# A two-layer transformer block on one Trainium2 core: scores issued before a step's weight units instead of after them

## The reference

```python
# first block: three families of 8 heads each on one qkv product
y_a = diff_attention(q_a, k_a, v_a, lam, lam_init, diff_subln[l])   # two softmaxes per head, p0 - lam * p1
y_b = stick_breaking_attention(q_b, k_b, v_b, sb_norm[l])           # suffix sums of log(1 - beta)
y_c = chunk_band_attention(q_c, k_c, v_c, rel_bias[l], ch_norm[l])  # softmax with a relative bias
x = x + jnp.einsum('bse,ed->bsd', jnp.concatenate([y_a, y_b, y_c], axis=-1), w_o[l])
x = x + jnp.einsum('bsf,fd->bsd', jax.nn.silu(g) * u, w_down[l])    # g: a width-3 convolution of h @ w_gate
# second block
a = mla_mixer(c_q, c_kv, k_rope, positions, ...)                    # 8 heads, keys of 128 + 64
bb = dsa_mixer(q_d, k_d, v_d, q_idx, k_idx, w_idx, positions)       # 8 heads over 64 selected keys
x = x + jnp.concatenate([a, bb], axis=-1) @ w_out[l]
x = x + memory_cross_attention(hc, mem_n, ...)                      # 4 heads over 256 memory rows
x = x + jnp.square(jax.nn.relu(hm @ w_up[l])) @ w_down[l]
```

## Time and profile before

| | us |
|---|---|
| median of 3 timed runs | 2481.21 (2480.41 to 2484.02) |
| the profiled execution, its own time | 2483.1 |
| its span, first to last instruction | 2481.3 |
| VectorE busy | 1500.9 (60%) |
| ScalarE busy | 1261.0 (51%) |
| mean granted clock of TensorE | 0.992 |

### The profile page before, as it was taken

How to read it: one execution, slowest core, us unless ns; L and a number is a source line. 1 busy time by engine, 2 the same in 40 slices (tenths; PEclk the granted TensorE clock), 3 DMA queues, 4 the chain that set the end, 5 groups by cost and what they waited for, 6 DMA issues and landing times.

```text
span 2481.3 us, 31755 instructions
## 1 busy us (share of the span) xinstructions
PE 2417.3 (97%) x12304; PEld 2020.1 (81%) x12304; DVE 1500.9 (60%) x2311; ACT 1261.0 (51%) x1974; POOL 5.2 (0%) x12
## 2 busy tenths in 40 slices
PE   6999999999999999999999999999999999999998
PEld 5888887788888888888877877787788888888886
DVE  5586777666666556645667544564666556556454
ACT  5466566655555435534556445555544444344343
POOL 0000000000000000000000000000000000000000
PEclk9999999999999999999999999999999999999999
DMA  6544444455555665565454544554566666666664
GB/s 211 174 162 158 136 154 147 150 188 177 197 180 191 189 189 187 192 205 185 155 180 144 178 128 134 173 169 136 160 179 193 189 187 184 194 185 191 206 187 141
DMA packets 118341, 432.11 MB, mean 174 GB/s; under 512 B 13184, under 2 KB 13328, under 8 KB 117680
## 3 DMA queue, kind: packets, MB, share of 16 engines
q1 hardware_dynamic: 117216, 424.70, 54.7%
q0 software_dynamic: 976, 5.39, 0.6%
HBM read 427.93 MB, written 2.11 MB: 173 GB/s over the span
## 4 chain that ended last, share of the span: by engine, by line
PE 94%; DVE 2%; ACT 2%; issue 1%; DMA 1%; ACTq 0%; SPq 0%; DVEq 0%
PE bank L428 29%; PE bank L437 15%; PE bank L439 15%; PE bank L438 15%; PE bank L430 15%; PE bank L612 1%; PE bank L454 1%; DVE lo_w L1177 1%; ACT hi_w L771 0%; PE bank L596 0%; PE bank L485 0%; DVE xT L1300 0%; PE bank L566 0%; PE bank L575 0%; PE bank L523 0%
## 5 line engine op out<-in xcount | busy, mean ns | idle before, releaser
L1177 DVE TENSOR_TENSOR lo_w<-raw_w,hi_w 128x1024 fp32r<-128x1024 f32 x804 | 968.1, 1219 | 689.8 <-ACT hi_w L771 689.0
L771 ACT ACTIVATE hi_w<-raw_w 128x1024 fp32r<-128x1024 f32 x804 | 834.0, 1053 | 678.7 <-PE bank L439 429.7
L428 PE MATMUL bank<-xT,hi_w 128*128 128x512 f32 x3008 | 1062.6, 398 | 2.9 <-DVE lo_w L1177 1.8
L430 PE MATMUL bank<-xT,lo_w 128*128 128x256 f32 x3008 | 843.6, 280 | 0.0
L428 PEld LDWEIGHTS bank<-xT,hi_w 128*128 128x128 f32 x3008 | 566.3, 188 | 139.0 <-issue 2.1
L430 PEld LDWEIGHTS bank<-xT,lo_w 128*128 128x128 f32 x3008 | 569.3, 189 | 0.2
L439 PE MATMUL bank<-hi_w,act_lo 128*128 128x512 f32 x864 | 341.2, 395 | 0.0
L438 PE MATMUL bank<-lo_w,act_hi 128*128 128x512 f32 x864 | 341.2, 395 | 0.0
L437 PE MATMUL bank<-hi_w,act_hi 128*128 128x512 f32 x864 | 341.2, 395 | 0.0
L437 PE MATMUL bank<-hi_w,xT 128*128 128x512 f32 (+1 forms) x736 | 295.0, 401 | 4.2 <-DVE xT L1300 3.4
L439 PE MATMUL bank<-hi_w,xT 128*128 128x512 f32 (+1 forms) x736 | 287.6, 391 | 0.0
(11 more groups left out here) (299 smaller groups left out, 1486.6 us busy)
## 6 DMA issues: line engine op xcount, KB each, us to landing
raw_w<-in_w_up SPq DMA_DIRECT2D x216, 512.0 KB, 4.2
raw_w<-in_w_down SPq DMA_DIRECT2D x216, 512.0 KB, 4.2
raw_w<-in_w_gate SPq DMA_DIRECT2D x88, 512.0 KB, 3.6
raw_w<-in_w_in SPq DMA_DIRECT2D x72, 512.0 KB, 3.8
raw_w<-in_w_qk SPq DMA_DIRECT2D x64, 512.0 KB, 3.6
raw_w<-in_w_v SPq DMA_DIRECT2D x32, 512.0 KB, 3.7
raw_w<-in_w_o SPq DMA_DIRECT2D x32, 512.0 KB, 3.6
raw_w<-in_w_out SPq DMA_DIRECT2D x32, 512.0 KB, 3.6
```

Source lines behind the costliest of these rows:

```text
L428: e.matmul(pair[c][:, :], w_hi[:, cols_k], both[:, kt].rearrange("p h t -> p (h t)"), start=(kt == 0), stop=False, skip_group_check=True)
L430: last = e.matmul(pair[c][:, 0:TOK], w_lo[:, cols_k], both[:, kt, 0, :], start=False, stop=(kt == g.kts - 1), skip_group_check=True)
L771: e.activation(hi_w[:, u % SPLIT_SLOTS, 0:unit_cols[u]], raw_w[:, u % RAW_SLOTS, 0:unit_cols[u]], ACT.Copy).then_inc(s["w_hi"], 1)
L1177: e.tensor_tensor(lo, raw_w[:, u % RAW_SLOTS, 0:unit_cols[u]], hi.bitcast(F32), ALU.subtract).then_inc(s["w_lo"], 1)
```

## The change

In the step of every family TensorE now issues its scores behind values and transposes, and the step's units after them. Only TensorE's program changes; the others run their steps as before. Step 15 of mla keeps its order, since its scores read keys that are transposed in that step.

```diff
@@ attend @@
                         turn_tiles("k_d", staging, 8)
-                    units(fill[step])
+                        units(fill[step])
+                        scores(family, step)
+                        continue
                     if step < n:
                         scores(family, step)
+                    units(fill[step])
@@ diff @@
                 if 3 <= step < 19:
                     diff_turn(step - 3)
-                units(2)
                 if step < 16:
                     diff_scores(step)
+                units(2)
@@ sb, first pass @@
             for step in range(NH):
+                sb_scores(step, False)
                 units(step % 2)
-                sb_scores(step, False)
@@ sb, second pass @@
                 if 2 <= step < NH + 2:
                     sb_suffix(step - 2)
-                units((2, 2, 3, 2, 2, 3, 2, 3, 2, 2, 3)[step])
                 if step < NH:
                     sb_scores(step, True)
+                units((2, 2, 3, 2, 2, 3, 2, 3, 2, 2, 3)[step])
```

## The result

| | before | after |
|---|---|---|
| median of 4 timed runs, us | 2481.49 (2480.41 to 2484.02) | 2492.31 (2490.78 to 2494.14) |
| the profiled execution, its own time | 2483.1 | 2490.78 |
| its span | 2481.3 | 2489.0 |
| mean granted clock | 0.992 | 0.994 |

A forecast was written before the change was run, and what follows sets the result against it. TensorE was taken to bound the kernel; 8.7 (diff) + 0.4 (sb) + 1.0 (mla) + 1.1 (cross) - 0.2 (dsa) = 11.0 us gave 2494.1 us by the profile, 2492.2 against the median, range 2485 to 2498.

The forecast's parts named there:

- The bound: Whole kernel: TensorE, busy 97% of the span, bounds it; each microsecond it newly waits is a microsecond of kernel.
- The reordering by itself is worth nothing.: Seams of all loops: about 0.2 us saved and 0.2 paid in row changes per step, net 0.
- Group ends: diff steps 4, 6, 8, 14: scores wait for VectorE's maxima behind its add, 1.24 us each, 5.0 in all.
- Step 2: diff step 2: with no values or turn as cover, scores wait 1.7 us for VectorE's maxima.
- Step 10: diff step 10, no group end: VectorE's late split delays the maxima, so scores wait 0.6 us.
- Step 12: diff step 12: values wait for ScalarE's copy of the v group, no longer covered by scores, +0.7 us.
- Odd steps: diff odd steps: 0.7 us for steps 1 and 3 together, 0 from step 5 on.
- sb's first pass: sb's first pass: S(3) waits 1.5 us for a tanh, one seam saved gives 1.0 back, net +0.4 us.
- Entries: First scores directly behind their producer's copy or add: mla +1.0 us, cross +1.1, band 0; dsa may gain 0.2.
- (a): Rival, chance 0.14: VectorE runs ahead and absorbs most diff waits; 4.6 us lost in all, 2485.8 us.
- (b): Rival, chance 0.06, faster: scores after turn free, sb saves its seam, waits for turned weights go; 2474.6 us.
- (c): Rival, chance 0.14: granted clock falls behind diff's stalls; two or three falls +4 us (2496), all +14 (2506).

The follow-up runs named there:

- the shifted loop: The whole change with diff and sb loops shifted one unit against the groups of units, on all engines: 2486.82 us, ratio 1.0018 against the kernel before.

## Why the prediction was right, by its steps

- **The bound.** TensorE's time is the kernel's: 7.1 us of new waits in diff and 10.8 us of time. VectorE and ScalarE are as busy as before (60% and 51%), and taking TensorE's waits away gave the time back.
- **"The reordering by itself is worth nothing."** Shown within 0.04 us a step: 0.65 us over the 16 steps of diff with VectorE one step earlier, 0.3 over band's 16 (0 predicted; it comes in even pieces of 0.02 a step), and + 0.8 us for the whole change with nearly every wait taken out. S starts 0.20 us behind the last transpose and not 0.11, the full price of a change of rows.
- **Group ends, four times 1.24.** Measured 1.34. VectorE's side was exact (E + 1.72); the step from its maximum to TensorE's start took 0.15 us, where I had put 0.05. Two experiments that change only the distance between the engines (one unit ahead, and VectorE one step earlier) remove the wait.
- **Step 2, 1.7.** Measured 1.77. What I had left to a rival, a fall of the clock, followed it in two of three profiles with this wait, and cost 1.5 us in each by the drift. How much of the median it carries stays open, since the timed runs beside the profiled one have no record of where their clock fell.
- **Step 10, 0.6.** Too large, 0.24 measured. VectorE's split ended at E - 0.07 and not at E + 0.26. TensorE's stalls before it had no part in that: from ScalarE's copy of the values to the end of the split it took 6.16 us in both kernels (158.00 to 164.16, 161.82 to 167.98). Two things of TensorE's order were left out. V stands directly behind the units, so its first pass takes 0.11 and not 0.21 us, as I had written under the reordering. And the seam of step 9 now holds scores of 256 columns where it held 128, so that E comes 0.19 us later (from E to the next unit matmul 1.28 us, where it was 1.09).
- **Step 12, 0.7.** Measured 0.90 from E to the values, less the 0.17 by which the same copy held them up before: 0.73.
- **Odd steps, 0.7 at steps 1 and 3.** Measured 0.22 and 0.10, and 0 from step 5. The odd steps are nearly free in the shifted loop too.
- **sb's first pass, + 0.4.** The stall was 1.45 (1.5 predicted). The first pass lost 0.4 on balance, as predicted, and both passes together 0.3.
- **Entries.** mla + 1.2 (1.0) and cross + 1.6 (1.1). The extra 0.3 in cross I had not seen: V(0) waits 0.31 us for ScalarE's copy of the turned weights, which stands behind the copy of the v_x group, with S(2) no longer there as cover. It is the same kind of wait as at step 12. dsa gained nothing (- 0.2 predicted).
- **Rivals.** (a) would have shown in diff as waits under 3 us: it had 7.1. (b) needed maxima before E + 0.1. (c) came true in two of three profiles, at the longest wait only, never at the four of 1.3 us. Two statements about it were off: the wait that the clock had answered, 2.27 us, was not twice but 1.3 times as long as the 1.7 of step 2, and by the prediction's own terms six stalls, not eight, had 1.2 to 1.7 us. A sum was off too: 1.72 us at 15 seams are 25.8 us, not some 20.

The sum predicted was 11.0; by drift it is 12.3, by the medians 10.8, with an interval of + 8 to + 14. The mechanism and the large terms held. That the forecast meets the median to 0.2 us is luck: steps 1, 3 and 10 were taken 0.7 us too large together, step 2, the group ends, band, mla, dsa and cross 1.6 too small, 0.6 us in small pieces of diff were not in the sum, and two profiles differ by 4.6 us where nothing was changed.

## What to carry to other kernels

When a block is moved ahead of filler work on the bounding engine, list for each thing it waits for how long behind the last filler that thing is ready; the loss is that time less what still stands in between, and it is paid only where both banks of a double buffer serve the same step or a producer stands directly ahead. Moving one engine's order by a step wants its partner's order moved too, or one filler left in between: either gave back all but 3 us here. Another engine's wait can also hide behind scores that TensorE has in work, so read the distance from E and not only the list of waits. And before shifting work about, look whether passes that use half of the rows can run in pairs: that was worth 14.5 us by the medians and 12.8 by the loops' drift, more than any order tried here.

## What the hardware showed that I had not expected

- Behind one wait of 1.71 us, ahead of which TensorE had been dense, the granted clock fell to 0.50 in two of three profiled executions, 0.6 and 1.5 us after the wait had ended, for 3.4 us each. It did not fall behind any of the waits of 1.27 us (four in each of the four profiled kernels that have them). At the entry of dsa, behind a wait of 2.27 or 2.28 us, it fell in nine profiles of twelve.
- The way from VectorE's accumulator read to TensorE's waiting matmul took 0.15 us (140.04 to 140.19). From ScalarE it took 0.15 us at S(3) of sb (240.90 to 241.05) and 0.05 us at the entry of mla (1412.36 to 1412.41). What makes the difference was not isolated.
- Two 64-row matmuls on opposite halves of the rows start 6 to 14 ns apart and take the time of one. A second one that comes 0.17 us late still overlaps: in the kernel before, S(1) and S(2) of sb's first pass start at 233.12 and 233.29, and the seam takes 1.08 us from E to the next unit matmul and not 0.95. In the one pair of sb that ran one behind the other, the second was held by a semaphore.
